# Gate rank and S5 kernel products on four column groups of TensorE, and S5 matrices copied out by two engines

## The reference, cut to what matters

```
h = x + 1/2 * SwiGLU(RMSNorm(x))
u = RMSNorm(h);  q, k, v, zg, r, us5 = split(u @ w_in)        # zg has 16 columns, the "gate rank"
log_a = log_sigmoid(zg @ w_gla_gate + b) / 16                 # 16 -> 256, decay of the gated linear attention
gated linear attention on q, k, v, log_a;   gate r
S5: 32 channel groups x 16 channels, 64 complex states each, x_t = A x_(t-1) + B u_t, y = Re(C x) + D u
h = h + concat(GLA out, S5 out) @ w_out;  then cross-attention, a second SwiGLU and a final norm
```

## Time and profile before

| | |
|---|---|
| time, median of 3 runs | 1355.11 us |
| time of the profiled execution | 1353.83 us |
| its span | 1351.9 us |
| TensorE busy (matrix products) | 1334.7 us, 99% |
| VectorE busy | 636.4 us, 47% |
| ScalarE busy | 420.9 us, 31% |
| GpSimd busy | 279.3 us, 21% |
| granted TensorE clock, mean | 0.999 |

### The profile page before, as it was taken

One profiled execution on the slowest core, in us unless ns is written; L12 is line 12 of the kernel. 1 busy time (PEld: TensorE's weight loads), 2 busy tenths in 40 slices (PEclk: granted clock), 3 DMA queues, 4 the chain that ended last, 5 costly groups with the idle time before them and its releaser, 6 DMA issues.

```text
span 1351.9 us, 24252 instructions
## 1 busy us (share of the span) xinstructions
PE 1334.7 (99%) x10659; PEld 1288.8 (95%) x10659; DVE 636.4 (47%) x790; ACT 420.9 (31%) x581; POOL 279.3 (21%) x387
## 2 busy tenths in 40 slices
PE   7999999999999999999999999999999999999997
PEld 6999999999999879999999997799999999999997
DVE  4545246643635525648665547344443244333333
ACT  6222122221224413465433223234221132212233
POOL 0000789988602202000002100030000000000011
PEclk9999999999999999999999999999999999999999
DMA  6533322232223341225432755232222322322221
GB/s 183 110 81 99 90 79 79 79 94 79 79 74 89 65 88 49 56 72 146 114 95 80 256 203 212 77 89 83 79 79 86 87 79 79 92 80 79 75 67 71
DMA packets 227049, 130.19 MB, mean 96 GB/s; under 512 B 22193, under 2 KB 221297, under 8 KB 226929
## 3 DMA queue, kind: packets, MB, share of 16 engines
q1 hardware_dynamic: 223072, 123.61, 31.9%
q10 hardware_dynamic: 3872, 5.04, 1.1%
HBM read 121.67 MB, written 5.78 MB: 94 GB/s over the span
## 4 chain that ended last, share of the span: by engine, by line
PE 95%; ACT 1%; DVE 1%; issue 1%; DMA 1%; SPq 0%; ACTq 0%; DVEq 0%
PE PS L638 92%; PE PS L1174 1%; DMA AR<-in_x_prompt 1%; PE PS L714 0%; ACT wh L1306 0%; ACT gua L1366 0%; DVE Hs L1890 0%; PE PS L1152 0%; PE PS L792 0%; PE PS L750 0%; PE PS L1125 0%; DVE AR L2190 0%; PE PS L803 0%; PE PS L857 0%; DVE wl L1672 0%
## 5 line engine op out<-in xcount | busy, mean ns | idle before, releaser
L1306 ACT ACTIVATE wh<-raw 128x1024 fp32r<-128x1024 f32 (+1 forms) x192 | 200.7, 1045 | 750.0 <-PE PS L638 749.9
L638 PE MATMUL PS<-xh,wh 128*128 128x288 f32 x1792 | 391.2, 300 | 0.1
L638 PE MATMUL PS<-xh,wl 128*128 128x288 f32 x1792 | 384.0, 296 | 0.0
L638 PE MATMUL PS<-xl,wh 128*128 128x288 f32 x1792 | 383.9, 296 | 0.0
L638 PEld LDWEIGHTS PS<-xh,wh 128*128 128x128 f32 x1792 | 288.0, 189 | 6.2 <-issue 5.0
L638 PEld LDWEIGHTS PS<-xl,wh 128*128 128x128 f32 x1792 | 289.0, 189 | 0.0
L638 PEld LDWEIGHTS PS<-xh,wl 128*128 128x128 f32 x1792 | 288.9, 189 | 0.0
L1672 DVE TENSOR_TENSOR wl<-raw,wh 128x1024 fp32r<-128x1024 f32 (+1 forms) x192 | 246.1, 1282 | 74.0 <-ACT wh L1306 72.8
L638 PE MATMUL PS<-yh,wh 128*128 128x288 f32 x960 | 206.4, 297 | 0.0
L638 PE MATMUL PS<-yh,wl 128*128 128x288 f32 x960 | 205.6, 296 | 0.0
L638 PE MATMUL PS<-yl,wh 128*128 128x288 f32 x960 | 205.6, 296 | 0.0
(11 more groups left out here) (313 smaller groups left out, 992.8 us busy)
## 6 DMA issues: line engine op xcount, KB each, us to landing
raw<-in_w_ffn_gu SPq DMA_DIRECT2D x88, 512.0 KB, 3.8
raw<-in_w_ffn_down SPq DMA_DIRECT2D x32, 512.0 KB, 4.0
raw<-in_w_in SPq DMA_DIRECT2D x16, 512.0 KB, 4.1
raw<-in_w_ckv SPq DMA_DIRECT2D x16, 512.0 KB, 3.8
raw<-in_w_ffn_down SPq DMA_DIRECT2D x16, 384.0 KB, 3.4
Hs<-in_cache_mem_k SPq DMA_DIRECT2D x6, 1024.0 KB, 6.4
raw<-in_w_out SPq DMA_DIRECT2D x8, 512.0 KB, 4.0
raw<-in_w_cq SPq DMA_DIRECT2D x8, 512.0 KB, 5.2
```

The lines of the kernel that those rows point to most:

```text
L638: return e.matmul(out, lhsT, rhs, start=start, stop=stop, **kw)
L1306: e.activation(wh[:, n % 2, 0:K * P], raw[:, n % 4, 0:K * P], ACT.Copy).then_inc(w_hi, 1)
```

## The change

The products of the gate rank and of the S5 kernel are put on four groups of 32 output columns of the array, that is on PSUM rows 0, 32, 64 and 96, with four neighbouring instructions on four different groups. The gate rank runs in two visits, after chunks 3 and 7 of block 4, with eight products each: group c takes chunk k0 + c, so the four groups hold four partial sums. Each product takes 32 weight columns, those of its own chunk and those of a neighbour, and the 16 unwanted rows meet zeros later: `wgate` is cleared and holds the gate weights four times, at rows 0, 32, 64 and 112, and the gate products contract all 128 rows, which adds up the four partial sums. The kernel products all run behind the transposes of round 1 and keep banks 6 and 7, one group of eight channel groups for each 32 rows. `Win` is copied in turns, even rounds by ScalarE from bank 4 and odd rounds by VectorE from bank 5, and `Kt` by VectorE after that, in four copies of 16 x 1024.

```diff
+        GATE_ROWS = (0, 32, 64, 112)
...
-                        e.dma_start(wgate[0:RANK, :], A["w_gla_gate"][0]).then_inc(S("d_gla"), 16)
+                        e.wait_ge(s_const, 7)
+                        for c in range(4):
+                            e.dma_start(wgate[GATE_ROWS[c]:GATE_ROWS[c] + RANK, :], A["w_gla_gate"][0]).then_inc(S("d_gla"), 16)
...
+            e.memset(wgate, 0.0).then_inc(s_const, 1)
...
                 if m == 1:
-                    e.wait_ge(S("win_ok"), 8)
+                    e.wait_ge(S("win_a"), 4)
+                    e.wait_ge(S("s5_v"), 4)
...
                 for r in range(8):
                     if r >= 2:
-                        e.wait_ge(S("win_ok"), r - 1)
-                        e.wait_ge(S("kt_ok"), r - 1)
+                        e.wait_ge(S(("win_a", "s5_v")[r % 2]), r // 2)
                     for j in range(4):
                         last = e.transpose(bank(4 + r % 2, P, at=j * P), WT[:, 4 * r + j, :, :].rearrange("p s q -> p (s q)"), ident)
                     last.then_inc(S("win_mm"), 1)
-                    for j in range(4):
-                        g = 4 * r + j
-                        last = mm(bank(6 + r % 2, P, at=j * P, rows=P5), Bb[:, g, :],
-                                  CA[:, g, 0:L5, :].rearrange("p j q -> p (j q)"))
-                    last.then_inc(S("kt_mm"), 1)
+                    if r == 1:
+                        for i in range(8):
+                            for q in range(4):
+                                g = 8 * q + i
+                                last = mm(PS[32 * q:32 * q + P5, 6 + i // 4, (i % 4) * P:(i % 4 + 1) * P], Bb[:, g, :],
+                                          CA[:, g, 0:L5, :].rearrange("p j q -> p (j q)"), skip_group_check=True)
+                        last.then_inc(S("kt_mm"), 1)
...
-            def gate_rank(k):
+            def gate_rank(k0):
-                if k == 0:
+                if k0 == 0:
                     e.wait_ge(S("wzg_ok"), 1)
-                    e.wait_ge(S("kt_ok"), 8)
+                    e.wait_ge(S("s5_v"), 8)
                 for j in range(2):
-                    last = mm(bank(6 + j, TH, rows=RANK), wzg[:, k, :], h[:, k, j * TH:(j + 1) * TH],
-                              start=k == 0, stop=k == KD - 1)
-                if k == KD - 1:
+                    for c in range(4):
+                        k = k0 + c
+                        pair = wzg[:, k - c // 3:k + 2 - c // 3, :].rearrange("p k r -> p (k r)")
+                        last = mm(PS[32 * c:32 * c + 32, 6 + j, 0:TH], pair, h[:, k, j * TH:(j + 1) * TH],
+                                  start=k0 == 0, stop=k0 == 4, skip_group_check=True)
+                if k0 == 4:
                     last.then_inc(S("zg_mm"), 1)
...
-                    e.wait_ge(S("d_gla"), 16 * 3)
+                    e.wait_ge(S("d_gla"), 16 * 6)
                 for j in range(2):
-                    last = mm(bank(4 + 2 * i + j, TH), wgate[0:RANK, i * P:(i + 1) * P], zg[0:RANK, j * TH:(j + 1) * TH])
+                    last = mm(bank(4 + 2 * i + j, TH), wgate[:, i * P:(i + 1) * P], zg[:, j * TH:(j + 1) * TH])
...
-                if b == 4:
-                    gate_rank(i)
+                if b == 4 and i in (3, 7):
+                    gate_rank(i - 3)
...
-            for r in range(8):
+            for r in range(0, 8, 2):
                 e.wait_ge(S("win_mm"), r + 1)
-                e.activation(Win[:, 4 * r:4 * r + 4, :], bank(4 + r % 2, 4, P), ACT.Copy).then_inc(S("win_ok"), 1)
+                e.activation(Win[:, 4 * r:4 * r + 4, :], bank(4, 4, P), ACT.Copy).then_inc(S("win_a"), 1)
...
-            for r in range(8):
-                e.wait_ge(S("kt_mm"), r + 1)
-                mark(CP(Kt[:, 4 * r:4 * r + 4, :], bank(6 + r % 2, 4, P, rows=P5)), "kt_ok")
+            for r in range(1, 8, 2):
+                e.wait_ge(S("win_mm"), r + 1)
+                mark(CP(Win[:, 4 * r:4 * r + 4, :], bank(5, 4, P)), "s5_v")
+            e.wait_ge(S("kt_mm"), 1)
+            e.wait_ge(S("win_a"), 4)
+            for q in range(4):
+                mark(CP(Kt[:, 8 * q:8 * q + 8, :], PS[32 * q:32 * q + P5, 6:8, :].rearrange("p b (i j) -> p (b i) j", j=P)), "s5_v")
...
-                    mark(TTT(two(zg[0:RANK, :]), PS[0:RANK, 6:8, 0:TH], two(R[0:RANK, :]), ALU.mult), "zg_ok")
+                    mark(TTT(two(zg), PS[:, 6:8, 0:TH], two(R[:]), ALU.mult), "zg_ok")
```

## The result

The changed kernel takes 1340.77 us, the median of four runs (1340.03 to 1341.63), beside 1355.14 for the kernel before. The ratio is 0.9897, 95% interval 0.988 to 0.9915. That is 14.4 us faster, where 13.4 were added up and 1341.2 us forecast. The profiled execution took 1341.45 us, with a span of 1339.4. Parts 1 and 4 of the page, which answer to the earlier trace rows: TensorE's busy time fell by 12.6 us, and its share of the chain that ended last stayed.

A forecast was written before the change was run, and what follows sets the result against it. TensorE, with 95% of the chain that ended last, was taken to bound the kernel. Gate rank 7.6 + S5 stage 5.8 = 13.4 us off gave 1340.4 (profiled) or 1341.7 (median); forecast 1341.2, likeliest's range 1338.5 to 1343.5, stated range 1338 to 1345.5.

The forecast's parts named there:

- The bound: Whole kernel: TensorE holds 95% of the chain that ended last, so shrinking its work shortens the kernel one for one.
- Gate rank: Block 4: two visits of 1.25 us replace eight that cost 10.1 us in all, 7.6 us less.
- S5 stage: S5 stage before block 0: kernel products take 2.0 us, then copies set the pace; 5.8 us less.
- Rival C: Both places: nothing overlaps and group changes cost nothing; gains only 0.4 and 1.6 us, 1353.1 us; chance 3%.
- Work moved behind: VectorE after round 7: four `Kt` copies of 1.225 us each cost nothing, under some 1.8 us of cover before block 2.
- Gate products: Block 10: calls may lose some 0.3 us each, but S5 outputs then wait longer for VectorE; counted 0.
- SyncE and GpSimd: Load queue: three more gate weight loads take 2.6 us and `wgate` is cleared early; counted 0.
- A: Both places: each change of column group empties the array, 0.13 us a change; 1359.4 us; chance 3%.
- B: S5 stage: the 16-column kernel products alone don't overlap, 8.0 us in place of 2.0; 1346.6 us; chance 5%.
- D: VectorE's `Kt` copies take twice the length, 3.1 us lost after the cover; 1344.3 us; chance 4%.
- E: S5 stage's last six rounds: granted clock falls from 2.4 to 1.2 GHz, about 2 us; 1343 us; chance 5%.
- The rule weighed against: Both places: at the skill's 3.07 times, products take about a tenth longer, 0.4 us in all.

The follow-up runs named there:

- experiment 1: Kernel before with only the gate rank's part of the change (two visits on four column groups), S5 stage as before: 1346.67 us, ratio 0.9944 to before.
- experiment 3: Kernel before with the gate rank in two visits of eight products, still on one column group with 16 weight columns: 1352.13 us, ratio 0.9984 to before.
- experiment 7: Changed kernel with the S5 transposes of rounds 2 to 5 put into banks 0 to 3 (six banks, not two): 1338.67 us, ratio 0.9887 to before.
- experiment 4: Changed kernel with the same products ordered group by group, not with neighbours on different groups: 1344.25 us, ratio 0.9925 to before.
- experiment 8: Changed kernel with ScalarE's second swap of the scanned states moved behind its weight split for block 11: 1340.15 us, ratio 0.9895 to before.
- experiments 9 and 10: Changed kernel with both six banks and the later swap, 1337.95 us; and the changed kernel unaltered beside it, 1340.59 us; kernel before there 1355.22.
- experiment 6: Changed kernel with ScalarE copying all eight rounds of `Win`, VectorE only the response matrices: 1339.85 us, ratio 0.9894 to before.

## Why the prediction was right

- **The bound.** TensorE's work and waits went one for one: 13.5 us less up to the end of the last block (1325.48 for the final norm's products, 1338.98 before).
- **Gate rank, 7.6 us.** Measured 7.5 (block 4, 16.42 to 8.88; experiment 1 alone 7.50 with the whole path). The sizing by columns from the earlier trace rows was right: 1.24 us a visit for 1.25. The split was a little off, by two errors that cancel: fewer ways in and out gave 1.79 us (experiment 3) where 1.6 were forecast, and the overlap 5.7 where the forecast implies 6.0. A record of 288 columns costs 0.24 us and not 0.25, so more of a visit was its way in and out.
- **S5 stage, 5.8 us.** Measured 6.0. Round 2 was put at 447.5 and came at 447.41, odd rounds at 448.45, 449.95 and 451.45 and came 0.2 us earlier (448.27, 449.79, 451.29), block 0 at 451.9 and came at 451.70. That the copies pace the stage was right, and experiment 7 shows it by taking the pace away. The choice of columns over the count of records was right too: 2.0 us, not 4.0 (445.28 to the round at 447.41, and 1.87 us in experiment 7, where nothing waits). Rival C gave regrouping without overlap only 0.4 us in this stage, as it took 8.0 us for the products one after another; by the estimate of experiment 4 they take 7.0 and it is worth about 1.5.
- **Work moved behind.** Four copies took 4.98 us, 4.9 expected: 1.22 us each and short gaps between them. VectorE's last `Win` copy came at 452.41, 0.3 us after the forecast, and of the 1.2 us ahead of the norm 0.77 were left. Block 2 did not wait. The further 0.6 us of cover was read a little small: the earlier trace rows give 471.77 - 471.04 = 0.73, and the trace after 0.72.
- **Gate products, 0.** Right, by the mechanism named: 0.76 us of gain against 0.78 us more waiting, and experiment 8 sets it free.
- **SyncE and GpSimd, 0.** The four loads of the gate weights take 2.62 us of the queue, and the weight load behind them is issued at 80.68 us, before at 80.78, so it was not even late. From the first norm's wait (32.5 us) to the S5 stage TensorE waits for nothing and takes 411.8 us in both traces.
- **The rivals.** C is out: the 16 records of a visit take 3.98 us on one group and 1.11 on four. A is out: the order that changes the group with every product is the fastest, 2.0 us against 4.15 and 5.83. B is out: the 64 records of 16-column products take 1.87 us where nothing waits, and 16 records one behind the other would take 1.7. D is out, with copies as sized. E did not happen at its place, with a clock of 1.00 over the stage and in the 24 transposes of experiment 7. The Trainium skill ("TensorE: Matmul & The Clock Gate", section Part 4, PE-mode transpose) says that transposes do not count as activity for the clock; no fall within this stage followed from it here, and no run here tests that rule by itself.
- **The rule weighed against.** The Trainium skill ("TensorE: Matmul & The Clock Gate", section Part 3, Packing small matmuls) gives 3.07 times for four row tiles and 2.38 for three column tiles, and nothing for four column tiles. Here the visit's 3.98 us on one group became 1.11, 3.6 times with the way out, more than either. The 0.4 us that were estimated from 3.07 are not there.
- **The number.** That 1341.2 lies 0.4 us from the measured 1340.77 is in part luck: the sum starts between two values for the kernel before that are 1.3 us apart, and the runs of one kernel spread over 1.6 to 2.4 us. What is borne out is the 13.4, to which the traces answer with 13.5. The medians give 14.4, and 14.6 beside experiments 9 and 10, 1.0 us and more above the forecast, which lies within the 95% interval of the ratio (11.5 to 16.3 us). The rivals' times are worked out from different starts, A and C from 1355.1 and B, D and E from 1354.6, which decides nothing.
- **What was not foreseen.** The second engine for the copies, which I took as it was, costs 0.7 us against one engine (experiment 6).

## What to carry to other kernels

Small-output fp32 products with 16 or 32 columns fit on four column groups at close to four times the rate, if neighbours in the program lie on different groups (two in a row on one group cost nothing in the gate visits); price them by columns from any four-group stretch in the same trace. When such products shrink, read what paces the stage next (here copies out of two banks) and ask for free banks before asking for a second engine (here 1.96 us gained against 0.7 lost). A gain that turns into a wait for another engine's chain may still be had: follow that chain back to the instruction that could stand behind another.

## What the runs showed of the hardware

- A fp32 product with 32 weight columns over 288 moving columns costs 0.14 us when four groups share the time (8 products, 16 records, 1.11 us with the way out), and one with 16 weight columns on one group 0.50 us (3.98 us for 8).
- Order within four groups: 32 products of 128 columns took 1.87 to 2.0 us with a new group each time, 4.15 in runs of four, 5.83 in runs of eight, and the next group started four records before the end of a run; runs of two cost nothing in the gate visits (1.13 against 1.11 us).
- Changing between the 128-column and the narrow form costs about 0.1 us each way and 0.1 us on the first products behind it; six visits less gave 1.79 us, 0.30 each.
- The time of VectorE's copy from PSUM went by the length, and hardly by the rows or the row offset: 16 x 1024 from rows 0, 32, 64 and 96 to row 0 took 1.21 to 1.23 us each (4.98 for the four with the gaps), 128 x 1024 before 1.225.
- The granted clock at the kernel's end differed between executions of one program (0.66 and 0.75 in windows over the last 11.4 us of the changed kernel's two traces), and with it the time of the last 14 transposes (3.25 and 2.43 us; 1.97 in the kernel before).
